# Even layer of a two-layer diffusion trunk as one program part: attention in 18 units beside the projections, output projection by row halves, norms from running squares

## The reference

```python
def _modulate(x, g, shift, scale):
    return _rms(x, g) * (1 + scale) + shift
...
qa, ka, va, qb, kb, vb = _split(h @ w_in, EVEN_WIDTHS)     # 4608 columns
...
a = jax.nn.softmax(s, axis=-1)
w = a[:, :, 0] - lam * a[:, :, 1]                          # differential attention
...
xp = xp + mod_p[2] * out_p
hp = _modulate(xp, norm2_g[l], mod_p[3], mod_p[4])
```

## Time and profile before

| | |
|---|---|
| median of 3 runs | 2898.34 us (2896.32 to 2904.95) |
| the profiled execution: time, and span of its core | 2901.56 us, 2899.8 us |
| granted TensorE clock, mean | 0.934 of full |
| PE busy | 2652.1 us (91%) |
| PEld busy | 2384.0 us (82%) |
| DVE busy | 1527.8 us (53%) |
| ACT busy | 1221.2 us (42%) |
| read from HBM | 601.38 MB, 209 GB/s over the span |

### The profile page before, as it was taken

How to read it: one execution, slowest core, us unless ns; L and a number is a source line. 1 busy time by engine, 2 the same in 40 slices (tenths; PEclk the granted TensorE clock), 3 DMA queues, 4 the chain that set the end, 5 groups by cost and what they waited for, 6 DMA issues and landing times. The chain is left out here.

```text
span 2899.8 us, 52317 instructions
## 1 busy us (share of the span) xinstructions
PE 2652.1 (91%) x20832; PEld 2384.0 (82%) x20832; DVE 1527.8 (53%) x1848; ACT 1221.2 (42%) x1488; POOL 0.5 (0%) x6
## 2 busy tenths in 40 slices
PE   6699956979999999999979998667979999999997
PEld 1388945868888888899978895565979999999996
DVE  0533345465545555476675342433575565657666
ACT  0233312324444444465544343132345555556553
POOL 0000000000000000000000000000000000000000
PEclk9899967989999999999989996686989999999998
DMA  9688700667888887865538861021535555555552
GB/s 389 261 315 309 301 18 0 262 232 290 308 316 306 312 319 302 319 233 189 189 109 316 318 204 45 17 90 36 188 124 187 185 189 187 188 189 189 184 194 82
DMA packets 171543, 608.33 MB, mean 210 GB/s; under 512 B 18680, under 2 KB 26872, under 8 KB 171128
## 3 DMA queue, kind: packets, MB, share of 16 engines
q1 hardware_dynamic: 170872, 603.12, 57.5%
q10 hardware_dynamic: 512, 2.97, 0.3%
HBM read 601.38 MB, written 4.63 MB: 209 GB/s over the span
## 5 line engine op out<-in xcount | busy, mean ns | idle before, releaser
L438 DVE TENSOR_TENSOR w_lo<-raw,w_hi 128x1024 fp32r<-128x1024 f32 x756 | 919.9, 1224 | 1010.7 <-ACT w_hi L431 1005.0
L431 ACT ACTIVATE w_hi<-raw 128x1024 fp32r<-128x1024 f32 x756 | 796.7, 1058 | 1146.5 <-PE banks L564 555.4
L562 PE MATMUL banks<-xs_ffn,w_hi 128*128 128x256 f32 x4224 | 1187.9, 281 | 15.6 <-DVE xs_ffn L699 14.7
L563 PE MATMUL banks<-xs_ffn,w_hi 128*128 128x256 f32 x4224 | 1180.4, 279 | 0.0
L564 PE MATMUL banks<-xs_ffn,w_lo 128*128 128x256 f32 x4224 | 1180.2, 279 | 0.0
L562 PEld LDWEIGHTS banks<-xs_ffn,w_hi 128*128 128x128 f32 x4224 | 796.2, 188 | 54.4 <-issue 29.0
L563 PEld LDWEIGHTS banks<-xs_ffn,w_hi 128*128 128x128 f32 x4224 | 796.4, 189 | 0.0
L564 PEld LDWEIGHTS banks<-xs_ffn,w_lo 128*128 128x128 f32 x4224 | 796.1, 188 | 0.0
L524 PE MATMUL banks<-raw,cond 128*32 128x512 f32 x1536 | 219.4, 604 | 28.4 <-PEq L594 17.2
L562 PE MATMUL banks<-xs_odd,w_hi 128*128 128x256 f32 (+2 forms) x640 | 181.9, 284 | 7.1 <-DVE xs_odd L699 7.1
L563 PE MATMUL banks<-xs_odd,w_hi 128*128 128x256 f32 (+2 forms) x640 | 179.9, 281 | 0.0
(11 more groups left out here) (275 smaller groups left out, 2390.7 us busy)
## 6 DMA issues: line engine op xcount, KB each, us to landing
raw<-in_w_mod SPq DMA_DIRECT2D x384, 512.0 KB, 5.8
raw<-in_ffn_w_up SPq DMA_DIRECT2D x352, 512.0 KB, 6.0
raw<-in_ffn_w_down SPq DMA_DIRECT2D x176, 512.0 KB, 3.8
raw<-in_even_w_in SPq DMA_DIRECT2D x72, 512.0 KB, 8.4
raw<-in_odd_w_in SPq DMA_DIRECT2D x64, 512.0 KB, 8.7
raw<-in_even_w_out SPq DMA_DIRECT2D x32, 512.0 KB, 8.7
raw<-in_odd_w_out SPq DMA_DIRECT2D x32, 512.0 KB, 4.2
raw<-in_odd_w_tail SPq DMA_DIRECT2D x8, 448.0 KB, 3.8
```

Of the source, the lines that this page charges most:

```text
L431: act.activation(w_hi[:, o % SPLIT], raw[:, s % RAW], ACT.Copy).then_inc(hi_done.sem, 1)
L438: dve.tensor_tensor(w_lo[:, o % SPLIT], raw[:, s % RAW], w_hi[:, o % SPLIT].bitcast(F32), ALU.subtract).then_inc(lo_done.sem, 1)
L562: pe.matmul(made, hi, x_hi, start=start and not second, stop=False, skip_group_check=second)
L563: pe.matmul(made, hi, x_lo, start=False, stop=False, skip_group_check=second)
```

## The change

- The first mod slabs, the even projection, the even attention and the output projection are one program part, one call of `project` with four phases.
- The even projection takes its nine column groups in the order 8, 6, 7, 0, 2, 4, 1, 3, 5 (keys and values of the grouped heads, their queries, then queries, keys and values of differential heads 0 to 3, then of heads 4 to 7), unrolled, and has eight mod groups that all use one bank, since banks 5 to 7 serve the attention.
- The attention is cut into 18 units of 512 score columns. A unit begins at an even slab s: PE's scores after slab s, DVE's maxima at s+1, ACT's exponentials, with row sums, at s+2, DVE's diagonal matrices with the inverse sums at s+3 and PE's transposing product with them after slab s+3, ACT's copy at s+4, PE's product with the values after s+4 or later. Units start at slabs 36 to 46, 48 to 58 and 64 to 74. Rotations, transposes and norms are 24 further entries of a table (with the value products 42), at fixed slabs from 12 to 86.
- The output projection is two phases of 16 slabs: the lower half of the rows (grouped heads), slabs 72 to 87, without mod slabs; then the upper half, slabs 88 to 103, with 32 mod slabs. Each half adds to `x`.
- All five norms take the sum of their squares from a running sum: with each residual half, ACT squares two tiles of `x` and DVE folds them into `sums` (for the first norm during the first mod slabs). At the norm PE sums over the partitions with two columns (`inverse_norm`), and gain and shift go from DVE to ACT. The input is made in eight parts, one per slab: three ahead (`LEAD`), five beside the first slabs (`act_at`, `dve_at`).
- POOL loads the key and value caches at the start of the part, and stores the new keys and values during it. POOL also copies and clears the second halves of the queries.

```diff
 KF = D_FF // P
 EVEN_TILES = 36
+EVEN_ORDER = (8, 6, 7, 0, 2, 4, 1, 3, 5)
 LAM_INIT = 0.8 - 0.6
...
@@ -183,16 +184,18 @@
 
 
 
-    def __init__(self, load, iters, groups, per_group, mods=0, iter0=0, by_halves=True):
+    def __init__(self, load, iters, groups, per_group, mods=0, iter0=0, by_halves=True, one_bank=False, after_one_bank=False):
         self.load, self.iters, self.groups, self.per_group, self.mods, self.iter0 = \
             load, iters, groups, per_group, mods, iter0
+        self.one_bank, self.after_one_bank = one_bank, after_one_bank
         self.seq = []
         for g in range(max(groups, mods)):
             own = [("own", g, k) for k in range(per_group)] if g < groups else []
             mod = [("mod", g, k) for k in range(MOD_SLABS)] if g < mods else []
             if own and mod:
-                for k in range(0, per_group, BATCH):
-                    self.seq += own[k:k + BATCH] + mod[k:k + BATCH]
+                run = MOD_SLABS * BATCH // per_group
+                for n in range(per_group // BATCH):
+                    self.seq += own[BATCH * n:BATCH * n + BATCH] + mod[run * n:run * n + run]
             else:
                 self.seq += own + mod
         self.slabs = len(self.seq)
...
@@ -360,9 +388,9 @@
         KS = KD // CHUNKS
         ph = {
             "mod": Phase(None, 4, 0, 0, mods=2),
-            "even_in": Phase(plain(ins["even_w_in"], 0, 2), 4, 2, KS, mods=2),
-            "even_in_end": Phase(plain(ins["even_w_in"], 8, 1), 1, 1, KS),
-            ("out", 0): Phase(plain(ins["even_w_out"], 0, 2), 2, 2, KS, mods=2),
+            "even_in": Phase(plain(ins["even_w_in"], 0, 9), 1, 9, KS, mods=8, one_bank=True),
+            ("out_b", 0): Phase(half_rows(ins["even_w_out"], KS // 2), 1, 4, KS // 2),
+            ("out_a", 0): Phase(half_rows(ins["even_w_out"], 0), 1, 4, KS // 2, mods=4, after_one_bank=True),
             ("up", 0): Phase(plain(ins["ffn_w_up0"], 0, 2), 2, 2, KS, mods=2),
...
+        PARTS, LEAD = KD // CHUNKS, 3
...
+            def modulate(act, b):
+                act.wait_ge(normed.sem, normed.at(b + 1))
+                for k in range(CHUNKS * b, CHUNKS * b + CHUNKS):
+                    for st in range(2):
+                        tile = h[:, k, T * st:T * st + T]
+                        made = act.activation(tile, tile, ACT.Identity, bias=shifts[:, k, st:st + 1],
+                                              scale=gains[:, k, st:st + 1])
+                made.then_inc(modulated.sem, 1)
+                act.wait_ge(modulated.sem, modulated.at(b + 1))
+                act.activation(xs[:, tiles(b), 0:NT], h[:, tiles(b)], ACT.Copy).then_inc(xs_hi.sem, 1)
...
+            def act_at(act, o):
+                if o + LEAD < PARTS:
+                    modulate(act, o + LEAD)
+
+            def dve_at(dve, o):
+                if o + LEAD < PARTS:
+                    multiply(dve, o + LEAD)
+                if o + LEAD <= PARTS:
+                    low(dve, o + LEAD - 1)
...
+            def add(dve, f, i, g):
+                for n in range(2):
+                    add_half(dve, f, i, g, n)
...
+            return ([square], [add, fold]) if last else ([], [add])
...
+                misc = [(12, "turn", ((VB, 0), (VB + 1, 0), (VB, 1), (VB + 1, 1)), 0), (25, "sums", 0, None),
+                        *((28 + n, "spread", (0, n), None) for n in range(5)),
+                        (33, "rope", (KB, 2), None), (34, "rope", (QB, 4), None), (35, "rope", (QB + 4, 4), None),
+                        (36, "rope", (QA, 4), 3), (41, "rope", (KA, 4), 4),
...
+                        (82, "sums", 2, None), (85, "spread", (2, 0), None), (86, "spread", (2, 1), None)]
...
+                def exponentials(act, u):
...
+                    for r in range(unit["rows"]):
+                        made = act.activation(e[:, s, keys * r:keys * r + keys], banks[:, SCORE_BANK, keys * r:keys * r + keys],
+                                              ACT.Exp, bias=neg[:, s, r:r + 1], scale=scale_of(unit),
+                                              accum_out=total[:, s, r:r + 1])
...
+                def turn_weights(pe, u):
...
+                    pe.wait_ge(diag_made.sem, diag_made.at(u + 1))
...
+                            mm = pe.matmul(out, e[:, s, keys * r + T * c:keys * r + T * c + T], dg[:, s, r],
+                                           start=n == 0, stop=n == terms - 1)
...
+                MIX_AT = ((4, 72), (5, 72), (6, 73), (7, 74), (0, 76), (1, 77), (2, 87), (3, 88))
...
+                def on_pool(pool):
+                    pool.dma_start(kv_cache[:, 0], ins["k_cache"]).then_inc(cache_in.sem, 16)
+                    pool.dma_start(kv_cache[:, 1], ins["v_cache"]).then_inc(cache_in.sem, 16)
```

More of the change, by code:

```diff
@@ L439, in split_lo, with split_stream @@
                               ALU.subtract).then_inc(lo_done.sem, 1)
-        def split_stream(eng, f, split, places, also=None, left=()):
+        def split_stream(eng, f, split, places, also=None, left=(), beside=None):
             owns = len(f.own_at)
@@ L449, in body @@
                         continue
+                    if beside and first:
+                        beside(eng, f.own_at.index(s))
                     ahead = f.own_at.index(s) + SPLIT
@@ L461, in split_stream @@
             rolled(eng, f.iters, body)
-            if not owns:
-                for o in range(SPLIT):
-                    split(eng, f.next, 0, o)
             return left_over(f, places)
@@ L511, in body @@
                     run_pieces(f, places, i, s, first, left)
+                    if beside and first and kind == "own":
+                        beside(pe, o)
             rolled(pe, f.iters, body)
@@ L684, in on_dve @@
+            def on_act(act):
+                if not spread:
+                    sum_act(act)
+                for b in range(LEAD):
+                    modulate(act, b)
+                    if between:
+                        between[0](act, b)
+                for b in range(LEAD, SPLIT if between else 0):
+                    between[0](act, b)
             def on_dve(dve):
-                for b in range(4):
-                    dve.wait_ge(A.sem, A.at(1 + b))
-                    dve.tensor_reduce(four_sum(b), four(h, b).rearrange("p k t -> p t k"), X_AXIS, ALU.add
-                                      ).then_inc(V.sem, 1)
+                wait(dve, mod_done.sem, spread)
@@ L713, in on_dve @@
-                low(len(PARTS) - 1)
-            def ready(pe, k):
-                b = max(n for n, (k0, _) in enumerate(PARTS) if k0 <= CHUNKS * k)
-                pe.wait_ge(V.sem, V.at(SPLIT_UP[b]))
-            return dict(act=on_act, pe=on_pe, dve=on_dve, steps=(10, 21, 1), ready=ready)
+                if not spread:
+                    sum_dve(dve)
+                for b in range(LEAD):
+                    multiply(dve, b)
+                    if b:
+                        low(dve, b - 1)
+                        if between:
+                            between[1](dve, b - 1)
@@ L739, in project, with steps, all_steps @@
         def project(phases, operands, act_pieces, dve_pieces, moving=(None, None, None, None), products=None,
-                    before=None):
+                    before=None, beside=None, start=0, mod_beside=()):
             before = before or {}
+            beside = beside or {}
+            def steps(n, name):
+                given = [b[name] for b in (before if n == start else {}, beside.get(n, {})) if name in b]
+                if not given:
+                    return None
+                def all_steps(eng, o):
+                    for one in given:
+                        one(eng, o)
+                return all_steps
             def ahead(name, eng):
@@ L748, in ready @@
                 kind, g, k = f.seq[f.own_at[o]]
-                if "ready" in before and f is phases[0] and isinstance(i, int) and i == 0 and g == 0:
+                if "ready" in before and f is phases[start] and isinstance(i, int) and i == 0 and g == 0:
                     before["ready"](pe, k)
+                for n, b in beside.items():
+                    if f is phases[n] and "ready" in b:
+                        b["ready"](pe, g, k)
                 if f is moving[0]:
@@ L807, in project @@
                 counted.advance(n)
+            if "over" in before:
+                before["over"]()
         def group_used(f, i, g):
@@ new lines, in residual_pieces, with add_half, fold, square @@
+        def residual_pieces(tb, sq, gate, first=0, last=True):
+            def add_half(dve, f, i, g, n):
+                q = i * f.groups + g
+                products_done(dve, f, i, g, n)
+                if first + q:
+                    dve.wait_ge(resid.sem, resid.at(first + 2 * q + n - 1))
+                tiles = slice(GROUP * q + 2 * n, GROUP * q + 2 * n + 2)
+                two = tb[:, 2 * n:2 * n + 2].rearrange("p t (s n) -> p t s n", s=2)
```

(17 more changed lines are left out.)

758 lines of the change are left out of this document (563 added, 195 removed).

## The result

The changed kernel takes 2965.58 us in the median of 4 runs (2964.85 to 2966.67), against 2898.34 before: ratio 1.0228, interval 1.0211 to 1.0246. It is 67 us slower where 59 us less were forecast, and it lies outside the range. The profiled execution took 2964.85 us, its span is 2963.0.

A forecast was written before the change was run, and what follows sets the result against it. PE was taken as the bound, starved only in places such as the even attention and norms. Gains of 52.3 (even layer's middle) and 6.6 (norms), 59 us off 2901.6, gave 2843, as median 2840; range 2803 to 2874.

The forecast's parts named there:

- The forecast's own sum: Whole kernel: 52.3 us off the even layer's middle and 6.6 off the norms, 59 together; chance 0.58.
- 0.116 us each, so a slab of 24 costs 2.79 us: PE's matmul records where nothing is in its way, 620 in 72 us; used to price PE's work.
- ACT splits slab o+4 at the end of slab o, and DVE after it: Attention units: splits take 1.06 + 1.22 us, DVE reaches slab o+1's work 2.4 us after slab o; PE waits 0 or 0.1.
- weights arrive in time: Even projection: PE's work accounts for the stage, and the DMA share is 0.79.
- 12.5 us of stalls: Even attention: uncovered waits at rotations, last units, differential norm, slab 72's split and slab 75's residual add; bounds 5 and 30.
- 7 at the output projection: Upper half: own slab's load waits for mod slabs, 6.7 us against PE's 4.6; 2.2 lost three times, 7 us.
- about 440: Even stage, first own product to last of the output projection: 237 + 108 + 65 + 30 us instead of 497.
- Rival 2: Attention units slip: each of 18 turnings waits 1.8 us for ACT's exponentials or table loads, 32 us more, 2872; chance 0.17.
- Rival 3: Even stage: clock falls; over 59 of 220 us at half clock cancels the gain, 40% gives 2928; chance 0.05.
- The norms: Five norms and end: first product at +12.0 not +20.7, parts every 5.5 us; gains 10.6, taken as 6.6 us.
- Rival 1: Norms: parts come as fast as PE asks, 39 us less, 2801; chance 0.15.
- The caches: First mod slabs: POOL's 1.3 MB share the DMA engines there, 0 to 3.2 us lost, 3.2 taken.

The follow-up runs named there:

- e2: Changed kernel with lam, rt and spare in one allocation, which moves all stage buffers back by 64 bytes: 2914.18 us, ratio 1.0057.
- e1: Kernel before, with 64 unused bytes per partition allocated ahead of the stage buffers: 2954.77 us, ratio 1.0194.
- e3: As e2, with SP loading each batch of own slabs of the even projection one batch earlier, ahead of waiting mod slabs: 2837.46 us, ratio 0.9786.
- e9: e3 with DVE multiplying one part further ahead at each norm: 2818.34 us, ratio 0.9726.
- e12: e9 with output-projection mod slabs spread over both halves, own loads one batch ahead there, POOL's cache loads after eight used own slabs: 2809.18 us, ratio 0.9686.
- e4: Kernel before with a different unused piece ahead of each stage's buffers (xs at 0, 192, 32, 64 past 256): matmul distances 117.5 to 119.1 ns.
- e10: Kernel before with xs at 96 (even layer, second net) or 128 (first net, odd layer) past 256: matmul distances 118.3, and 119.9 / 119.3 ns.
- e11: Kernel before with the 64 unused bytes ahead of all tiles, so weights and stage buffers move together: 2903.68 us.

## Why the prediction was wrong

- **The forecast's own sum** (59 us less than before) rested on PE's cadence being untouched: "0.116 us each, so a slab of 24 costs 2.79 us". In the changed kernel it is 2.88. I had read the distance off the trace as a constant of the operation. No rival had it, and nothing in the diff's logic shows it: three small tiles moved `xs`. Cost 51 us by e2, 56 by e1. Which tile in front counts, and why, stays open.
- **"ACT splits slab o+4 at the end of slab o, and DVE after it"** is the step that failed in the attention. It holds only if the slab has landed. The page said that it had not: the group of L431 has 131.2 us of idle time before it that ended with a load of `even_w_in`. I took "weights arrive in time" from PE being busy and from the DMA share of 0.79, and overlooked that they arrived late for ACT, which cost nothing as long as nothing but splits stood in its queue. The change put the units there. The wait itself did not grow, 131 us before and after. I had also read 3.8 us for a load to land off the row of `ffn_w_down`, where `even_w_in` has 8.4. Where the sum had 12.5 us of stalls, and 7 at the output projection, PE was idle for 81.7 us (e2), with the half clock behind the gaps. With the order of loads mended, the sum nearly holds: 451.2 us from first to last own product in e3 against "about 440". Of the 11 us left, 4 are the gaps at the output projection, 4.1, 3.4 and 3.4 us where 2.2 each stood in the sum. With the address and the order both mended, e3 takes 2837 us where 2840 were forecast. That it comes so near is in part luck, since single terms are off both ways.
- **Rival 2** had the right place, PE's wait at the turnings, and a wrong cause: 1.8 us at each of 18 would be 32 us, and six turnings waited 4.9 us each, 29.4 together, which is near it by luck. Six other small products waited 3 to 4.5 us. What stood ahead was not exponentials or table loads but the late split in DVE's and ACT's queues.
- **Rival 3** was a side effect. The stage's clock was 0.92, not below 0.9; the half clock followed the gaps (85 us of it in 535, 73 of them with PE busy, so at most 37 us lost, where the rival needed 59) and mostly went with them in e3 (21 us in 451). The Trainium skill (TensorE: Matmul & The Clock Gate, HAM oscillation — how this bites in real kernels) describes a matmul kernel in which waits for DMA between groups of matmuls bring the clock down again and again. The trace agrees, with the wait for DMA passed on to PE through ACT and DVE: 81 us at half clock with the late loads (e2), 21 without (e3).
- **The norms** were right: from last product to the ninth slab 58.3, 48.0 and 46.1 us against 53.8, 49.9 and 47.0 before, so +4.5, -1.9 and -0.9 where +4.2, -1.1 and -0.3 were forecast, before the 1 us that the sum takes off at each norm (the longer distance between matmuls puts 0.6 us into each measured value). Even layer, from the last turning on, 44.7 against 51.7, so -7.0 where -4.4 was forecast; end -8.5 against -9.0. Rival 1 would have had them all short; the order of the queues forbade it, and e9 shows what DVE's part of that order was worth, 19 us.
- **The caches**: 3.2 forecast, 2.8 by the trace of the change, 3.1 by e12.
- **Small slips in the sum**, which change nothing: the waits listed under "not covered" add up to 11.4 to 12.4 and not 12.5, and the terms of rival 1 to 36 us and not 39.

## What to carry to other kernels

Before work is put into a queue, look what the instruction ahead of it waits for: an engine that stands idle at a load costs nothing until something useful stands behind it, so read the idle column of every queue that gets new work, not that of the bound engine alone. Loads that wait for nothing should be issued ahead of loads that wait for PE. And after any change of allocations, compare the distance between matmuls in a steady stretch with the one before, before reading anything else.

## What the hardware showed that I had not expected

The distance from one 256-column matmul to the next, weights loaded anew for each, depends on where the moving operand lies in the partition relative to the tiles in front of it, the weights among them: 116.7 to 120.0 ns over eight positions 32 bytes apart, at full clock, where PE waits for nothing (e1, e4, e10), and when all tiles move together it stays at 116.7 in all stages but the second net, with 117.8 there (e11). 64 unused bytes cost 56 us of this kernel (e1). With the same distances the second net, and the odd layer's output projection, took either 116.7 or 117.8 ns from kernel to kernel, without a cause that these runs name.
